# Moving the spatial half of an even mixer between the steps of its attention

## The reference

```python
mod = (c_act @ ada_w[l] + ada_b[l]).reshape(bsz, 6, 1, D_MODEL)
sh1, sc1, g1, sh2, sc2, g2 = (mod[:, i] for i in range(6))
h = rms_norm(x, norm1_g[l]) * (1.0 + sc1) + sh1
# even mixer
u, v, q, k, vd = split_cols(h @ w_in, (SGU_WIDTH, SGU_WIDTH, DIFF_QK, DIFF_QK, DIFF_V))
a_out = spatial_gating(gelu(u), gelu(v), ...)        # u * (causal W_s @ layer_norm(v) + b_s)
b_out = differential_attention(q, k, vd, lam, subln_g, lam_init)
y = concatenate([a_out, b_out], axis=-1) @ w_out
x = x + g1 * y
h = rms_norm(x, norm2_g[l]) * (1.0 + sc2) + sh2
x = x + g2 * grouped_moe(h, router_w, router_b, moe_w_gu[l], moe_w_down[l])
```

## Time and profile before

| | us |
|---|---|
| median of 3 runs | 1073.78 |
| lowest, highest | 1069.72, 1075.07 |
| profiled execution | 1065.87 |
| its span in the trace | 1063.9 |
| TensorE matmul busy | 935.1 |
| TensorE weight load busy | 609.6 |
| VectorE busy | 416.1 |
| ScalarE busy | 171.2 |
| GpSimd busy | 13.0 |

### The profile page before, as it was taken

One profiled execution on the slowest core, in us unless ns is written; L12 is line 12 of the kernel. 1 busy time (PEld: TensorE's weight loads), 2 busy tenths in 40 slices (PEclk: granted clock), 3 DMA queues, 4 the chain that ended last, 5 costly groups with the idle time before them and its releaser, 6 DMA issues.

```text
span 1063.9 us, 13148 instructions
## 1 busy us (share of the span) xinstructions
PE 935.1 (88%) x5454; PEld 609.6 (57%) x5454; DVE 416.1 (39%) x984; ACT 171.2 (16%) x416; POOL 13.0 (1%) x51
## 2 busy tenths in 40 slices
PE   2699789499999899896999989987769999999994
PEld 2385554475556455452868777764356555555551
DVE  4846575442131311311796754543251111111112
ACT  2121120221111011102101422340111111111101
POOL 1000000000000000000000000000000000000000
PEclk9999789689999999898999989957859999999998
DMA  9996644647999999999377331170209799999941
GB/s 353 387 382 238 226 158 158 237 184 295 408 405 409 404 408 408 405 399 378 120 263 286 130 118 54 70 313 1 79 13 407 306 409 408 409 408 409 409 164 41
DMA packets 96079, 294.13 MB, mean 276 GB/s; under 512 B 2448, under 2 KB 3088, under 8 KB 96016
## 3 DMA queue, kind: packets, MB, share of 16 engines
q1 hardware_dynamic: 95184, 289.89, 70.7%
q10 hardware_dynamic: 688, 2.82, 0.7%
q0 software_dynamic: 144, 0.52, 0.1%
HBM read 292.18 MB, written 1.05 MB: 276 GB/s over the span
## 4 chain that ended last, share of the span: by engine, by line
PE 50%; issue 26%; DVE 11%; DMA 6%; SPq 4%; ACT 3%; POOL 0%; DVEq 0%; POOLq 0%
PE bank L618 13%; PE bank L614 9%; PE bank L801 9%; DMA ring<-w_gu_dram 4%; DVE gb L1190 4%; SPq L406 4%; PE bank L816 3%; PE bank L792 3%; PE bank L647 2%; PE bank L669 2%; PE bank L830 2%; PE bank L546 2%; PE bank L566 1%; DMA ring<-ada_w_dram 1%; PE bank L554 1%
## 5 line engine op out<-in xcount | busy, mean ns | idle before, releaser
L801 PE MATMUL bank<-ring,scr 128*64 128x256 f32 x2176 | 253.7, 387 | 9.4 <-DMA ring<-w_gu_dram 9.4
L801 PEld LDWEIGHTS bank<-ring,scr 128*64 128x64 f32 x2176 | 155.0, 139 | 102.2 <-issue 20.8
L618 PE MATMUL bank<-hT,ring 128*128 128x256 f32 x640 | 145.7, 389 | 0.0
L618 PEld LDWEIGHTS bank<-hT,ring 128*128 128x128 f32 x640 | 124.2, 196 | 17.9 <-issue 0.5
L816 PE MATMUL bank<-ring,scr 128*64 128x512 f32 x544 | 122.6, 592 | 0.0
L1190 DVE SCALAR_TENSOR_TENSOR gb<-ring,small,gb 128x512 f32<-128x512 f32 x140 | 105.5, 754 | 5.0
L1640 DVE TENSOR_TENSOR scr<-bank,scr 128x256 f32<-128x256 f32 x34 | 14.4, 424 | 205.3 <-ACT scr L1130 205.3
L792 PEld LDWEIGHTS bank<-scr,xh 128*128 128x128 f32 x576 | 71.6, 203 | 24.5 <-issue 22.0
L792 PE MATMUL bank<-scr,xh 128*128 128x128 f32 x576 | 77.8, 292 | 2.3 <-DVE scr L1612 2.3
L816 PEld LDWEIGHTS bank<-ring,scr 128*64 128x64 f32 x544 | 38.9, 137 | 64.4 <-issue 59.8
L1112 ACT ACTIVATE scr<-bank 128x256 f32<-128x256 f32 (+1 forms) x52 | 23.4, 450 | 300.5 <-PE bank L809 237.7
(11 more groups left out here) (215 smaller groups left out, 684.3 us busy)
## 6 DMA issues: line engine op xcount, KB each, us to landing
ring<-w_gu_dram SPq DMA_DIRECT2D x64, 2048.0 KB, 21.6
ring<-w_down_dram SPq DMA_DIRECT2D x32, 2048.0 KB, 21.4
ring<-ada_w_dram SPq DMA_DIRECT2D x24, 2048.0 KB, 17.6
ring<-od_w_in_dram SPq DMA_DIRECT2D x9, 2048.0 KB, 14.2
ring<-ev_w_in_dram SPq DMA_DIRECT2D x5, 2048.0 KB, 17.4
ring<-ev_w_out_dram SPq DMA_DIRECT2D x2, 2048.0 KB, 9.7
ring<-od_w_out_dram SPq DMA_DIRECT2D x2, 2048.0 KB, 11.0
xs<-x_dram ACTq DMA_DIRECT2D x1, 1024.0 KB, 5.8
```

Of the source, the lines that this page charges most:

```text
L618: ins = pe.matmul(banks[h][:, m * 256:(m + 1) * 256], w[:, c, (2 * h + m) * P:(2 * h + m + 1) * P], x_part[:, c, :], start=(c == 0 and m = ...
L801: ins = pe.matmul(b[64 * m:64 * m + 64, 256 * u:256 * u + 256], h[:, c, :], w[:, c, 512 * u + 256 * m:512 * u + 256 * m + 256], start=(fir ...
```

## The change

The spatial product leaves its place behind the attention. At the second F TensorE now does fills 8 and 9, the spatial product (into banks 2 and 3) and sum 8; at the third F the transposes of `uu` and the fills 10 and 12, the spatial half's part of the output projection; at the fourth the sums 9 and 10. Behind the attention stand both halves of the gate rows, the transposes of `vg`, the fills 11 and 13 and sum 11. ScalarE's Gelu of u and its copies of the transposed `uu` move to the same F places. VectorE finishes the spatial half in step 4 between `combine(3)` and `sub_norm_scale(0)`, and the `ada` work moves with it. `ada_out(0, 11)` moves out of the mixer into the second norm, behind `rstd_of`. In the order of panels out0 and out1 now stand ahead of ada9. The amount of arithmetic is the same.

```diff
--- before.py
+++ after.py
@@ -124,7 +124,7 @@
 
 
 PRE = [[("ada", 0), ("ada", 1), ("ada", 2), ("ada", 3), ("in", "v"), ("in", "q"), ("ada", 4), ("ada", 5), ("in", "k"),
-        ("in", "vd"), ("ada", 6), ("ada", 7), ("in", "u"), ("ada", 8), ("ada", 9), ("out", 0), ("out", 1),
+        ("in", "vd"), ("ada", 6), ("ada", 7), ("in", "u"), ("ada", 8), ("out", 0), ("out", 1), ("ada", 9),
         ("ada", 10), ("ada", 11)],
        [("in", "gate"), ("ada", 4), ("in", "a"), ("ada", 5), ("in", "v"), ("ada", 6), ("ada", 7)]
        + [("in", n) for n, _ in OD_ORDER[3:7]] + [("ada", 8), ("in", "q2"), ("in", "k2"), ("ada", 9), ("ada", 10),
@@ -687,29 +687,34 @@
                 pe.wait_ge(*emptied(0, 3))
                 pe.wait_ge(qz_zero, 1)
                 pe.wait_ge(*emptied(0, 5))
-                attention(0, 0, [[lambda: (fill(0, 6), fill(0, 7), ada(6), ada(7))],
-                                 [lambda: fill(0, 8)], [lambda: fill(0, 9)]])
-
-                pe.wait_ge(score_out, 6)
-                pe.wait_ge(vn_ready, 2)
-                for t in range(T):
-                    for g in range(4):
-                        ins = pe.matmul(bank[4 + t][:, g * P:(g + 1) * P], wT[:, g, :], vn[:, t, g * P:(g + 1) * P],
-                                        start=True, stop=True)
-                    ins.then_inc(sgu_mixed, 1)
-                ada(8)
-                for feats, made in ((uu, aout_ready), (vg, bout_ready)):
+                def spatial():
+
+                    pe.wait_ge(vn_ready, 2)
+                    pe.wait_ge(*emptied(0, 7))
+                    for t in range(T):
+                        for g in range(4):
+                            ins = pe.matmul(bank[2 + t][:, g * P:(g + 1) * P], wT[:, g, :], vn[:, t, g * P:(g + 1) * P],
+                                            start=True, stop=True)
+                        ins.then_inc(sgu_mixed, 1)
+
+                def turned(feats, made):
                     for t in range(T):
                         pe.wait_ge(made, t + 1)
                         transposes([feats[:, t, c * P:(c + 1) * P] for c in range(4)])
-                        if t == 0:
-                            gate_rows(0, 0, (0,) if feats is uu else (1,))
+
+                def first_out():
+                    turned(uu, aout_ready)
+                    pe.wait_ge(turn_free, turn.n)
+                    fill(0, 10)
+                    fill(0, 12)
+
+                attention(0, 0, [[lambda: (fill(0, 6), fill(0, 7), ada(6), ada(7))],
+                                 [lambda: (fill(0, 8), fill(0, 9)), spatial, lambda: ada(8)], [first_out],
+                                 [lambda: (ada(9), ada(10))]])
+                gate_rows(0, 0)
+                turned(vg, bout_ready)
                 pe.wait_ge(turn_free, turn.n)
-                fill(0, 10)
                 fill(0, 11)
-                ada(9)
-                fill(0, 12)
-                ada(10)
                 fill(0, 13)
                 ada(11)
                 gate_row2(0)
@@ -1043,12 +1048,15 @@
                     ins.then_inc(fill_act[0], 1)
                 act.wait_ge(lam_part, 1)
                 act.activation(lam_t[:, 2:4], lam_t[:, 0:2], ACT.Exp).then_inc(lam_exp, 1)
-                attention(0, 0, [])
-                for h in range(2):
-                    wait_fill(act, 0, 8 + h)
-                    act.activation(uu[:, h, :], fill_bank(8 + h)[:, :], ACT.Gelu_apprx_tanh).then_inc(fill_act[0], 1)
-                for k in range(4):
-                    mixed_T(k, 4 * (k // 2), k % 2)
+
+                def u_out():
+                    for h in range(2):
+                        wait_fill(act, 0, 8 + h)
+                        act.activation(uu[:, h, :], fill_bank(8 + h)[:, :], ACT.Gelu_apprx_tanh).then_inc(fill_act[0], 1)
+
+                attention(0, 0, [[], [u_out], [lambda: mixed_T(0, 0, 0), lambda: mixed_T(1, 0, 1)]])
+                for k in range(2, 4):
+                    mixed_T(k, 4, k % 2)
 
             def empty_odd(f):
                 _, name, h = FILLS[1][f]
@@ -1242,6 +1250,8 @@
                 if ph:
                     rstd_of(ph)
                 if s == 1:
+                    if l == 0:
+                        ada_out(0, 11)
                     gate_row2_out()
                 dve.wait_ge(x_ready, ph + 1)
                 for c in range(4):
@@ -1355,39 +1365,42 @@
                     dve.tensor_copy(vv[:, h, :], fill_bank(6 + h)[:, :]).then_inc(fill_dve[0], 1)
                 ada_out(0, 6)
                 ada_out(0, 7)
+
+                def spatial_out():
+                    for t in range(T):
+                        dve.wait_ge(sgu_mixed, t + 1)
+                        dve.wait_ge(fill_act[0], 5 + t)
+                        for g in range(4):
+                            o = uu[:, t, g * P:(g + 1) * P]
+                            ins = dve.scalar_tensor_tensor(out=o, in0=bank[2 + t][:, g * P:(g + 1) * P],
+                                                           scalar=col[:, C_SGUB + g:C_SGUB + g + 1], in1=o,
+                                                           op0=ALU.add, op1=ALU.mult)
+                        ins.then_inc(aout_ready, 1)
+
                 for j in range(2, 6):
+                    if j == 4:
+                        ada_out(0, 8)
                     scores(0, j, j, sc, nm_ev[:, 1, :], 0)
                     combine(j - 1, j - 1)
                     if j == 3:
                         sub_norm(0)
+                        ada(8)
                     if j == 4:
+                        spatial_out()
                         sub_norm_scale(0)
-                        ada(8)
                 combine(5, 5)
+                ada(9)
+                ada(10)
                 sub_norm(1)
-                ada_out(0, 8)
-                for t in range(T):
-                    dve.wait_ge(sgu_mixed, t + 1)
-                    dve.wait_ge(fill_act[0], 5 + t)
-                    for g in range(4):
-                        o = uu[:, t, g * P:(g + 1) * P]
-                        ins = dve.scalar_tensor_tensor(out=o, in0=bank[4 + t][:, g * P:(g + 1) * P],
-                                                       scalar=col[:, C_SGUB + g:C_SGUB + g + 1], in1=o,
-                                                       op0=ALU.add, op1=ALU.mult)
-                    ins.then_inc(aout_ready, 1)
-                gates_out(0, (0,))
                 sub_norm_scale(1)
-                gates_out(0, (1,))
-                ada(9)
+                ada_out(0, 9)
+                ada_out(0, 10)
+                gates_out(0)
                 residual(0, 10, 0)
-                ada(10)
                 residual(0, 10, 1)
-                ada_out(0, 9)
                 ada(11)
                 residual(0, 10, 2)
-                ada_out(0, 10)
                 residual(0, 10, 3)
-                ada_out(0, 11)
 
             def odd():
                 step(dve.memset(glu[:, :, 0:TAPS - 1], 0.0))
```

## The result

| | median, us | runs | lowest, highest |
|---|---|---|---|
| kernel before | 1069.94 | 8 | 1068.6, 1075.56 |
| changed kernel | 1081.76 | 8 | 1079.05, 1085.71 |

The ratio is 1.0105, 95% interval 1.0081 to 1.013: the change costs 11.8 us, where 9.5 were forecast. The profiled execution of the changed kernel took 1085.71 us, the slowest of its eight; that of before took 1065.87, less than any of its eight.

What follows compares the result with a forecast made beforehand. The even mixer's chain, mostly TensorE's, was taken to set when the full expert stage starts. Passage, stall and moved work +10.3, ada9/ada10 -3.1, fill starts -0.65 +1.3, tail +1.8, last addition -0.2: +9.5 us, 1083.3; range 1075 to 1090.

Steps and rivals of the forecast that it cites:

- The sign that was named: In the new trace, at the expert stage's start: the first expert matmuls come near 231 us.
- Fills 8 and 9 together: Joined in the mixer, the second fill pays no slow start: some 15.2 us, a gain of 0.65.
- The new stall ahead of fill 10: TensorE's second transposes wait for ScalarE's copy, queued behind exponentials that wait for VectorE's late scores: 5.7 us.
- Fills 10 and 12: Spatial half's output projection in the mixer: 14.0 us plus a slow start of 0.65, bounds 0 and 1.25.
- The passage: From the last attention step to fill 11: jobs queue on bank 7 behind VectorE, 14.0 us for 12.0 before.
- Fills 11 and 13: Last output fills of the mixer: 14.0 us plus a slow start of 0.65, bounds 0 and 1.25.
- The tail: At the mixer's end, residuals 2 and 3 wait for VectorE's ada(11), done later than fill 13: +1.8 us.
- The last sum in the norm: With ada_out(11) behind rstd_of, gate_row2 just fits ahead of the second norm's transposes: 0, or 1 us if it slips.
- A shift arrives whole: The expert stage has no room, so a shift at the second norm's squares reaches the end whole: +9.5 us.
- (2): Bank 7's jobs hide behind the second half's norm, no measurable change: passage 8.0 us, total +3.5, 1077.3; chance 0.15.
- (3): Faster: the mixer really overlaps and both fill pairs start at full clock: -1.2 us at most, 1072.6; chance 0.07.
- (4): Slower by more: slow fill starts, gate_row2 slipping, late panels at the expert stage: +15 us, 1088.8; chance 0.13.

Runs made afterwards that it cites:

- the kernel before with filler: Kernel before with 6 unread matmuls on TensorE between logits and ranks, in both layers: ratio 0.9982.
- the third experiment: Changed kernel with VectorE's ada(11) ahead of the first residual instead of between residuals 1 and 2: 1079.87 us, ratio 1.0096.
- the second and third experiment: The second: changed kernel with VectorE taking out modulation sums 9 and 10 ahead of sub_norm_scale(1), not behind it: 1079.59 us, ratio 1.0078.
- the first edit: Changed kernel with ScalarE's two copies of the turned uu ahead of the exponentials of step 5: 1079.4 us, ratio 1.009.
- the four edited kernels: Changed kernel with early uu copies, early sums 9 and 10, or early ada(11), singly and all together: ratios 1.009, 1.0078, 1.0096, 1.0019.
- the three edits: Changed kernel with uu copies ahead of exponentials, sums 9 and 10 ahead of the scale, ada(11) ahead of the first residual; together 1071.82 us, ratio 1.0019.
- the rearranged kernel: Changed kernel with early uu copies and ada(11), early gate rows, spatial product behind A2, vg transposes first, sum 9 ahead of the scale: 1059.5 us, ratio 0.9916.
- one kernel built on the one before: Kernel before with both halves of the first gate's rows made in banks 0 and 1 between sums 6 and 7: 1066.43 us, ratio 0.9978.
- The delay experiment: Kernel before with 12 further copies on VectorE between the last residual and the second norm's opening: 1076.31 us, ratio 1.0085.
- its filled twin: Kernel before with the 12 added VectorE copies plus 6 unread TensorE matmuls behind gate_row2: 1073.14 us, ratio 1.0044.
- the filler: Rearranged kernel with unread TensorE matmuls, 4 ahead of gate_row2 and 6 per layer between logits and ranks: ratio 0.9902.

## Why the prediction came out right, point by point

The sign, the place and the size within its own range were right: 11.8 us measured, 9.5 forecast with +7 to +12 as the likeliest case's own range, and 1081.76 us in 1075 to 1090. How near the size came is in part luck, in three ways.

- The sum itself fell short. In the pair of traces the squares come 13.0 us later after fill 8's start (84.8 us for 71.8), not 9.5: fills 10 and 12 are 1.0 over, the passage 1.5, fills 11 and 13 1.1. With the norm and the routing it is 15.9. The sign that was named, the first expert matmul near 231, was missed: 240.0, or 237.3 without the scatter ahead of fill 8. The medians lie closer together than this pair, whose one trace is the slowest of its eight and whose other is faster than any of its eight.
- The base of 12.0 us for the old passage is one draw. In three other traces of the same program it is 9.4. In those, fill 13 takes 8.81 us for 7.11, so of the difference 2.1 us are left from fill 8 to the squares (69.7 us, 118.44 to 188.17, in the kernel before with filler, for 71.8).
- The forecast of 1083.3 us stands on a median of three runs, 1073.78. On the median of eight, 1069.94, it would be 1079.4.

Term by term:

- **Fills 8 and 9 together**: 15.2 forecast, 15.11 measured. Right. In the third experiment the same block began at full clock (1.00 in its first 3 us, for 0.56) and took 13.73, so the start at the lower level is not a fixed price.
- **The new stall ahead of fill 10**: 5.7 forecast, 6.4 measured (6.6 and 5.0 in the second and third experiment), its chain as told (spatial_out, scale, scores, exponentials, copy). From T3 to fill 10, where that chain runs, 8.4 were forecast and 8.38, 8.38 and 8.24 measured; the rest is how soon A3 ends. Shown by the first edit, which brought the stall to 2.7 and the 8.38 to 4.28.
- **Fills 10 and 12**: 14.65 forecast; 15.61, 15.65 and 16.65 in the traces that keep the stall, 14.00 in the four without it. The stall also lets the clock fall ahead of the block (0.50 in its first 2 us), which I had priced at 0.65 and which was 1.6 to 2.65. Mis-sized: I took the row of fill 9 where the bound at fill 8 (1.25) was nearer, and even that was too low.
- **The passage**: 14.0 forecast, 15.1 to 15.5 in three traces. The order of waits was right; the groups of rows took 2.08 us, not 1.92, and the second sum 1.86, not 1.16, at a clock of 0.56 in the passage. Mis-sized by 1.1 to 1.5 us.
- **Fills 11 and 13**: 14.65 forecast, 15.71 measured; 14.00 (twice) to 17.00 in the four edited kernels. Mis-sized by 1.1 us; the others lie from 0.65 under the forecast to 2.35 over it.
- **The tail**: +1.8 forecast, 1.9 shown by the third edit. Right.
- **The last sum in the norm**: 0 forecast; no difference that can be told, and the transposes stand where they stood. Right.
- **A shift arrives whole**: right behind the first expert matmul. Ahead of it, in norm and routing, the changed kernel takes 34.5 us for 31.6, and this 2.9 us is in no term of my sum. With one or all of the three edits it is 33.4 to 33.6, in the rearranged kernel 31.1, and one kernel built on the one before has 33.6 too; so how much of the 2.9 belongs to the change stays open. The delay experiment and its filled twin speak for the clock after idle time as the cause.
- **Rivals**: (2) and (3) did not come. The mechanism of (2) was right in itself: with the gate halves out of the passage and the two sums between the transposes it fell to 6.8, in the rearranged kernel. (4)'s late panels cost nothing that can be seen: TensorE had no idle time ahead of the first expert matmul, and behind it there are 843.6 us for 842.6.
- **A reading of the earlier trace rows**: the first slice of the first long stage, and the second of the other, show 7 tenths of DMA, not nine. Nothing in the sum hangs on it.

The row of fill 8, applied to each pair behind a wait, would have given +10.7, nearer to the 11.8 than my row of fill 9. In the trace the fills behind the stall and behind the passage do begin at the lower level (0.50 in their first 2 us). That agrees with the Trainium skill (TensorE: Matmul & The Clock Gate, What's actually happening), which says that activity releases the throttle. The gather behind the filler, 0.54 after TensorE had been busy, is not foreseen by that sentence alone. A price per start is a range, and one row does not give it.

Moving work forward was to fill TensorE's waits. It did not, because it was put ahead of a step (T2) whose idle time lies inside the step (ahead of T3), and because it brought two queues with it: ScalarE's copy behind exponentials, and four jobs in a row on one bank.

## What to carry to other kernels

When work is moved between the steps of another chain, follow its hand-overs too: who copies its result out, and what stands ahead of that copy in that engine's order. The loss was in one copy behind two exponentials, one addition behind a scale and one accumulation ahead of a residual, and in the lower clock behind the waits that they made, not in the work itself. A buffer that is handed over in turn turns independent small jobs into a chain; give those whose data are ready early another bank, and place them in a wait that is there already. Before a stretch of one trace serves as a base, see how long it is in other executions of the same program: the 12.0 us here were 9.4 in three others, and a gain expected from hand-overs came from the clock.

## What was not expected of the hardware

- 2.0 us of matmuls put into a wait of 2.8 us ahead of sum 7 kept the granted clock at 0.93 to 1.00 in the 7 to 8 us behind it, in three traces of three; the ten traces without them have 0.50 to 0.52 there. The same 29 records took 4.39 us for 8.20.
- Filler matmuls until 3.8 us ahead of a gather, with small matmuls between, did not: the gather ran at 0.54 and took 6.73 us.
- A delay of 5.5 us on another engine cost 9.1 us (1.0085, interval 5.7 to 12.5 us), and TensorE's clock was 0.52 of full on average in the 35 us behind it; before it was 0.64. That the one comes from the other is supported by the filled twin, not shown.
- The same block of 32 records at the same place of the program took 13.73 us in one trace and 15.1 to 15.2 in four others, by the level at which it began; the last two fills 14.00 to 17.00. This is as large as the terms one wants to measure, and the runs of one kernel scatter by 6 us and more.
- A copy of 128x512 within SBUF on VectorE took 0.46 us (5.49 for 12), one out of PSUM 0.69.
